# Attention stages of a six-block network: ScalarE's exponentials ahead of its copy of the turned probabilities

## The reference

```
proj = rmsnorm(x) @ w_in                     # queries, keys, values of all three kinds
out_c: 4 heads, softmax(map 1) - lambda * softmax(map 2), times values   # 8 maps
out_b: 6 heads, softmax(q k / sqrt(96)), times values                    # 6 maps
out_a: 6 heads, three dilated bands, folded into one mask of logarithms  # 6 maps
x = x + concat(out_a, out_b, out_c) @ w_o
```

## Time and profile before

| | before |
|---|---|
| median of 3 runs | 1948.38 us |
| the profiled execution | 1947.71 us |
| its span in the trace | 1945.7 us |
| granted TensorE clock, mean | 0.998 |
| busy: PE, DVE, ACT | 1915.8, 1296.4, 985.5 us |
| share of the chain that ended last: PE, DVE, ACT | 88%, 6%, 2% |

### The profile page before, as it was taken

The page is one execution under the profiler, slowest core; times in us unless marked ns, Lnnn a source line. Parts: engine busy times, 40 slices in busy tenths (PEclk is TensorE's granted clock), DMA queues, the critical chain, the costliest instruction groups (busy, mean ns, idle before and its releaser), DMA issues.

```text
span 1945.7 us, 25832 instructions
## 1 busy us (share of the span) xinstructions
PE 1915.8 (98%) x10477; PEld 1612.6 (83%) x10477; DVE 1296.4 (67%) x1719; ACT 985.5 (51%) x1300; POOL 73.6 (4%) x108
## 2 busy tenths in 40 slices
PE   8999999999999999999998999999999999999998
PEld 7878888878887887888887888889888888788887
DVE  6967666966666675586669575667766667557664
ACT  6655445765444445454466554454544453445443
POOL 0100000100000000001000000000000000000000
PEclk9999999999999999999999999999999999999999
DMA  7426664435654754466643366545566565455651
GB/s 255 152 87 218 193 195 136 165 109 191 190 192 131 264 174 151 141 217 194 195 163 109 109 219 192 195 162 189 190 205 188 192 213 182 153 160 192 191 185 61
DMA packets 204469, 340.52 MB, mean 175 GB/s; under 512 B 5749, under 2 KB 143489, under 8 KB 204352
## 3 DMA queue, kind: packets, MB, share of 16 engines
q1 hardware_dynamic: 202464, 332.00, 52.9%
q10 hardware_dynamic: 1888, 6.89, 1.0%
HBM read 337.81 MB, written 1.05 MB: 174 GB/s over the span
## 4 chain that ended last, share of the span: by engine, by line
PE 88%; DVE 6%; ACT 2%; issue 1%; POOL 0%; DVEq 0%; ACTq 0%
PE ps L598 18%; PE ps L600 18%; PE ps L599 18%; PE ps L738 17%; PE ps L736 10%; PE ps L735 2%; DVE w_lo L1845 1%; PE ps L615 1%; DVE arena L2329 1%; PE ps L1092 1%; PE ps L1171 0%; DVE arena L2114 0%; PE ps L880 0%; PE ps L907 0%; PE ps L1131 0%
## 5 line engine op out<-in xcount | busy, mean ns | idle before, releaser
L1845 DVE TENSOR_TENSOR w_lo<-w_raw,w_hi 128x2048 fp32r<-128x2048 f32 x299 | 690.2, 2312 | 244.7 <-ACT w_hi L1304 244.3
L1304 ACT ACTIVATE w_hi<-w_raw 128x2048 fp32r<-128x2048 f32 x301 | 574.3, 1912 | 79.8 <-PE ps L600 64.1
L738 PE MATMUL ps<-xT,w_hi 128*128 128x512 f32 x1400 | 499.3, 396 | 0.0
L736 PE MATMUL ps<-xT,w_lo 128*128 128x256 f32 x1600 | 413.5, 279 | 0.0
L598 PE MATMUL ps<-w_hi,u_h 128*128 128x512 f32 (+1 forms) x1032 | 404.6, 392 | 4.0 <-DVE u_l L2271 1.1
L600 PE MATMUL ps<-w_hi,u_l 128*128 128x512 f32 (+1 forms) x1032 | 399.3, 387 | 0.0
L599 PE MATMUL ps<-w_lo,u_h 128*128 128x512 f32 (+1 forms) x1032 | 399.2, 387 | 0.0
L736 PEld LDWEIGHTS ps<-xT,w_lo 128*128 128x128 f32 x1600 | 301.6, 189 | 16.3
L738 PEld LDWEIGHTS ps<-xT,w_hi 128*128 128x128 f32 x1400 | 262.8, 188 | 54.3
L598 PEld LDWEIGHTS ps<-w_hi,u_h 128*128 128x128 f32 x1032 | 193.7, 188 | 44.7 <-issue 3.3
L600 PEld LDWEIGHTS ps<-w_hi,u_l 128*128 128x128 f32 x1032 | 193.7, 188 | 40.1
(11 more groups left out here) (257 smaller groups left out, 1853.7 us busy)
## 6 DMA issues: line engine op xcount, KB each, us to landing
w_raw<-mlp_w_dram SPq DMA_DIRECT2D x128, 1024.0 KB, 5.7
w_raw<-ret_w_in_dram SPq DMA_DIRECT2D x48, 1024.0 KB, 5.2
w_raw<-w_up_dram SPq DMA_DIRECT2D x32, 1024.0 KB, 5.7
w_raw<-w_down_dram SPq DMA_DIRECT2D x32, 1024.0 KB, 4.9
w_raw<-w_in_dram SPq DMA_DIRECT2D x16, 1024.0 KB, 5.2
w_raw<-ret_w_out_dram SPq DMA_DIRECT2D x16, 1024.0 KB, 4.9
w_raw<-cf_w_pw_dram SPq DMA_DIRECT2D x12, 1024.0 KB, 5.2
w_raw<-sc_w_in_dram SPq DMA_DIRECT2D x12, 1024.0 KB, 5.2
```

Source lines behind the costliest of these rows:

```text
L736: pe.matmul(ps[:, bank, 0:S], w_lo[:, slot, wsl], xT_h[:, kc, :], start=False, stop=False)
L738: ins = pe.matmul(ps[:, bank, :], w_hi[:, slot, wsl], both, start=False, stop=kc == KC - 1)
L1304: act.activation(w_hi[:, slot, :], w_raw[:, slot, :], ACT.Copy).then_inc(hi_ready[slot], 1)
L1845: tt(w_lo[:, slot, :], w_raw[:, slot, :], w_hi[:, slot, :].bitcast(F32), ALU.subtract).then_inc(lo_ready[slot], 1)
```

## The change

In ScalarE's part of every stage, the copy of the turned probabilities of map s-3 moves from ahead of the exponentials of map s-1 to behind them. Its two waits move with it. Nothing is added or removed, and no other engine's program is changed.

```diff
--- before.py
+++ after.py
@@ -1501,13 +1501,6 @@
                         act.wait_ge(feed_T.sem, feed_T.at(sec, 1))
                         act.activation(u_h[:, 0, :, :].rearrange("p a b -> p (a b)"), ps[:, 4, :], ACT.Copy,
                                        scale=gain("subg", sec.layer, 0)).then_inc(feed_hi.sem, 1)
-                    m = map_at(s - 3)
-                    if ends_set(m):
-                        e = set_of(m)
-                        act.wait_ge(pT_ready.sem, pT_ready.at(sec, e + 1))
-                        if e >= 3:
-                            act.wait_ge(pv_ready.sem, pv_ready.at(sec, pv_of(e - 3) + 1))
-                        act.activation(pT[:, e % 3, :], ps[:, 6, 0:384], ACT.Copy).then_inc(pT_sb.sem, 1)
                     m = map_at(s - 1)
                     if m is not None:
                         act.wait_ge(max_ready.sem, max_ready.at(sec, m + 1))
@@ -1517,6 +1510,13 @@
                             ins = act.activation(sm[:, m % 4, c], sm[:, m % 4, c], ACT.Exp, bias=negmax[:, j:j + 1], scale=-1.0,
                                                  accum_out=zsum[:, j:j + 1])
                         ins.then_inc(probs_ready.sem, 1)
+                    m = map_at(s - 3)
+                    if ends_set(m):
+                        e = set_of(m)
+                        act.wait_ge(pT_ready.sem, pT_ready.at(sec, e + 1))
+                        if e >= 3:
+                            act.wait_ge(pv_ready.sem, pv_ready.at(sec, pv_of(e - 3) + 1))
+                        act.activation(pT[:, e % 3, :], ps[:, 6, 0:384], ACT.Copy).then_inc(pT_sb.sem, 1)
                     m = map_at(s - 4)
                     if m is not None and m >= C_MAPS and m % 2:
                         i = pv_of(set_of(m))
```

## The result

The changed kernel took 1953.2 us, the median of 8 runs (1951.24 to 1954.98); the kernel before took 1948.3 us in 8 runs (1946.89 to 1950.89). The ratio is 1.0026, 95% interval 1.0017 to 1.0035: slower, by 4.9 us in the medians. The forecast was 1952.6. The span of the profiled execution grew from 1945.7 to 1952.0 us, and this execution was the slowest of the eight.

What follows compares the result with a forecast made beforehand. PE, busy 98% of the span, bounds the kernel. Net delays of PE sum to 2.11 us a block; 2 x 2.11 = 4.2, on the median 1948.38, gives 1952.6 us; own range 1951.4 to 1954.0, wider range 1949.0 to 1955.5.

Steps and rivals of the forecast that it cites:

- its own range: Whole kernel: the range of the forecast by itself, without the rivals, 1951.4 to 1954.0 us.
- The 1.42 us from exponentials to reader: PE's reader of a moved copy can't start before the exponentials' start + 0.89 + 0.48 + 0.05 us.
- The gain of stage 4: Early in each block, exponentials ahead of the copy bring the maxima PE awaits at 71.75 earlier: -0.24 us a block.
- loss in stage 7: PE's reader L914 in stage 7 starts at 72.82 instead of 72.32: PE loses 0.50 us, net +0.26.
- Seven waits a block: PE's L907 and L914 would show some seven idles of 0.2 to 0.55 us a block, waiting for the copy.
- The squares and L1494: On ScalarE behind the late copy: squares 0.87 us late in stages 15 and 16, L1494 1.27 late in stage 17.
- PE's busy time: Whole kernel: PE's busy time would stay as before.
- Rival A: PE's readers stand far enough behind, so the late copy is hidden: 1947.9 us, not slower; chance 0.07.
- Rival B: PE pays the delay once, about 0.5 to 1 us a block, later stages have slack: 1950.4 us; chance 0.22.
- Rival C: ScalarE becomes the bound, the copy's 0.37 us adding up in more stages: +8, 1956.4 us; chance 0.10.
- Rival D: Short idles drop PE's clock to 1.2 GHz: at least 17.8 us more a block, about 1984 us; chance 0.01.

Runs made afterwards that it cites:

- the late stages alone: The kernel before, with the copy moved behind the exponentials only in stages 11 to 20: 1951.91 us, ratio 1.0019 to the kernel before.
- the filled kernel: The changed kernel plus two spare 256-column matmuls on TensorE in the idle of stage 5: 1952.0 us, ratio 1.0020 to the kernel before.
- the early stages alone: The kernel before, with the copy moved behind the exponentials only in stages 4, 6, 8 and 10: 1949.9 us, ratio 1.0010.
- stage 4 alone: The kernel before, with the copy moved behind the exponentials only in stage 4: 1948.51 us, ratio 1.0004 to the kernel before.

## Why the prediction was right

The time lay 0.6 us from the forecast and inside its own range, for the forecast's reason in the main. The prediction gave 0.51 to slower, with 0.2% as the least that counts. It is about as close as that: the interval of 1.0017 to 1.0035 holds 1.0020. The delay of PE within a block, forecast and as measured in the second block (its rows less 361.65, against the rows of before less 56.73):

| place | forecast | measured |
|---|---|---|
| stage 7, L914 | 0.26 | 0.12 |
| stage 11, L907 | 0.50 | 0.46 |
| stage 13, L907 | 1.04 | 1.11 |
| stage 15, L907 | 1.22 | 1.30 |
| stage 16, L907 | 1.39 | 1.47 |
| stage 17, L907 | 1.68 | 1.78 |
| stage 21, L907 | 2.11 | 2.24 |

- **The 1.42 us from exponentials to reader** held for the value matmuls L914 (370.82 to 372.24). For the transposes L907 it was 1.50 to 1.51, as they start 0.14 us behind the end of the copy and not 0.05, which I had read from the scores behind L1494. The clearest check of the mechanism is stage 11 with the weight half put ahead, 0.95 more. Rows of ScalarE and PE in the second block of the changed kernel, for stages 15, 17 and 21:

```profile
403.14 0.40 ACT L1510 ACTIVATE arena<-arena,st 128x128 f32<-128x128 f32 x1 [1.21 <-DVE st L2114]
404.64 0.52 PE L907 MATMUL ps<-ident,arena 128*128 128x128 f32 x3
...
410.37 0.60 ACT L1494 ACTIVATE arena<-ps 128x512 f32<-128x512 f32 x1
410.87 0.40 ACT L1510 ACTIVATE arena<-arena,st 128x128 f32<-128x128 f32 x1
...
423.71 0.40 ACT L1510 ACTIVATE arena<-arena,st 128x128 f32<-128x128 f32 x1 [2.08 <-DVE st L2114]
```

- **The gain of stage 4** was 0.33 us, not 0.24. VectorE's L2094 is idle for 0.24 before, but an instruction of VectorE that needn't wait starts 0.08 ahead of the recorded end of the one before it (370.71 + 1.22 = 371.93, the next at 371.85 in the changed kernel), and this comes on top.
- **Luck** has a part in the 0.6 us. The greater gain, and a somewhat smaller loss in stage 7, made the forecast too high by 0.14 us a block at first. By the end of the block it was too low by 0.13, to which the 0.08 more of the readers L907 adds. And it had nothing for the clock.
- **Seven waits a block**, 0.2 to 0.55 us each: seven of 0.17 to 0.46 us have a row in the second block. Stage 15, forecast with 0.18, has no row with idle, but its reader too starts 1.50 behind the exponentials and PE's delay there grew by 0.19, so it was held.
- **The squares and L1494** behind the late copy: for the squares it is shown by putting them ahead. For L1494 the rows speak, with no experiment of its own: the exponentials of stage 17 start right behind it, with no idle, at 49.22 us of the block where 49.20 was forecast.
- **PE's busy time** was to stay as before and grew by 3.4 us, through the clock.
- **Rival A** fell with the first row of PE waiting for the copy. **Rival B** fell with the late stages alone, 1.85 us a block. **Rival C**, 8 us, fell too: in each attention block PE waits for L1494 once, in stage 5, where it did before, and nowhere for w_lo.
- **Rival D**, given 0.01, is the step that was mis-sized. I read from one execution that the clock holds over a longer idle, and priced its fall at 17.8 us a block. It fell in both profiles of the changed kernel, in the first block alone, and cost 1.07 us net, since part of the slow work lay where PE would have waited: stage 7's wait of 0.41 has no row in that block. My estimate from rows left out that a fall can be short and partly covered. The kernel that I weighed against it, of which the Trainium skill tells ("TensorE: Matmul & The Clock Gate", section "A second HAM failure mode: psum-queue depth-cycling"), was the better guide. The later traces agree with it in part: behind short idles the clock fell in 9 of the 28 attention blocks profiled, once in each and not again and again.

The sum of waits alone, 4.6 us, would be 0.24%; the 1.0020 of the filled kernel, 3.9 us, lies a little below it, within its interval. The kernel before has falls of the clock in its own runs, which make its median higher. At a granted clock of 0.999 both kernels have a few runs: 1951.2 and 1951.1 us for the changed one, and 1946.6 on average for three of the kernel before, timed beside the early stages alone. That is 4.6 us, though not on the same chip.

## What to carry to other kernels

When an instruction is moved back on an engine, work out two times for each place: when its reader starts against when it can now be ready, and who waits for what now stands behind it. Exponentials that wait for their input anyway gain nothing by going first. Where TensorE idles for a few tenths of a microsecond up to one, and most of all twice within a few microseconds, look at the granted clock of several executions before calling the idle free. Matmuls that compute nothing can be worth having there: they took 1.1 us off the changed kernel, went with a ratio of 0.9989 instead of 1.0004 for stage 4 alone (on another chip), and changed nothing in the kernel before.

## What was not expected of the hardware

- The granted clock fell to 1.2 GHz behind idles of 0.85 and 0.38 us, of 0.80 and 0.41, and once of 0.79 with 0.5 some 17 us earlier. In the other block of the same execution it stayed at 2.4 GHz behind nearly the same idles, except with the copy at the end of each stage, where it fell in both. What decides between them no run here shows.
- The price is in the rows: 0.43 us from one 512-column matmul to the next instead of 0.23, and 1.0 to 3.1 us in a block where it fell.
- The waits for the copy repeat to 0.03 us from one execution of the changed kernel to the next and from one block to the next, but for the one in stage 7 that a fall covers. The wait for L1494 differs more, 0.85 and 0.79. The time of the changed kernel varies by 3.2 us in nine runs and by 3.7 in eight, and by 1.2 in eleven with the spare matmuls in it. Positions in the trace told effects of 0.3 us apart that the times of these rounds did not.
